# First norm of a two-block transformer kernel computed on token rows, with the raw tokens turned later

## The reference, cut to what matters

```python
def rmsnorm(x, g):
    xf = x.astype(jnp.float32)
    y = xf * lax.rsqrt(jnp.mean(xf * xf, axis=-1, keepdims=True) + EPS)
    return (y * g.astype(jnp.float32)).astype(x.dtype)
...
    h = jnp.concatenate([meta, x, zeros])        # 16 + 256 rows of 1024
    xn = rmsnorm(h, norm_mix_g[l])
    proj = xn @ w_in[l]                          # sb q,k,v and df q,k,v
    ...
    gates = sigmoid(xn @ w_gate[l] + b_gate[l])
    h = h + merged @ w_out[l]                    # needs the raw h again
```

## Time and profile before

| | us |
|---|---|
| median of 3 runs | 1934.32 (1933.79 to 1935.63) |
| profiled execution, its own time | 1935.6 |
| its span, first to last instruction | 1934.0 |
| TensorE busy | 1830.3 |
| VectorE busy | 799.9 |
| ScalarE busy | 595.1 |
| first matmul of unit 0 starts | 27.91 |

### The profile page before, as it was taken

How to read it: one execution, slowest core, us unless ns; L and a number is a source line. 1 busy time by engine, 2 the same in 40 slices (tenths; PEclk the granted TensorE clock), 3 DMA queues, 4 the chain that set the end, 5 groups by cost and what they waited for, 6 DMA issues and landing times.

```text
span 1934.0 us, 27605 instructions
## 1 busy us (share of the span) xinstructions
PE 1830.3 (95%) x11191; PEld 1225.8 (63%) x11192; DVE 799.9 (41%) x1359; ACT 595.1 (31%) x952; POOL 34.5 (2%) x61
## 2 busy tenths in 40 slices
PE   5999999989998999999999999999999999999996
PEld 5777878989998899899844344344344343343442
DVE  4344655868885554546422122122122122122222
ACT  4665777443434455565410000000000000000001
POOL 1000000000000000000000000000000000000000
PEclk8999999989998999999889999999999999999998
DMA  6323334768883744435849999999999999999994
GB/s 211 127 96 109 110 109 152 253 206 266 280 313 118 253 156 153 164 120 175 300 182 418 428 428 428 429 428 429 429 428 428 429 428 428 428 428 429 428 428 209
DMA packets 147813, 568.65 MB, mean 294 GB/s; under 512 B 6016, under 2 KB 102376, under 8 KB 123040
## 3 DMA queue, kind: packets, MB, share of 16 engines
q1 hardware_dynamic: 139616, 536.60, 70.5%
q0 software_dynamic: 8128, 31.07, 4.7%
HBM read 566.58 MB, written 3.43 MB: 295 GB/s over the span
## 4 chain that ended last, share of the span: by engine, by line
PE 58%; DMA 33%; ACT 4%; DVE 3%; issue 1%; SPq 0%; DVEq 0%
DMA s_ring<-in_w_mlp 33%; PE banks L2024 10%; PE banks L1644 9%; PE banks L1646 8%; PE banks L1645 8%; PE banks L1783 3%; PE banks L1784 3%; PE banks L1785 3%; PE banks L2061 3%; PE banks L2034 2%; PE banks L1611 1%; PE banks L2009 1%; ACT r_w2h L703 1%; DVE s_W L1066 1%; DVE r_w2l L1087 1%
## 5 line engine op out<-in xcount | busy, mean ns | idle before, releaser
L2024 PE MATMUL banks<-s_ring,s_W 128*64 128x512 f32 x2048 | 460.9, 598 | 29.8 <-DMA s_ring<-in_w_mlp 29.8
L2024 PEld LDWEIGHTS banks<-s_ring,s_W 128*64 128x64 f32 x2048 | 139.1, 137 | 332.3 <-issue 258.0
L1027 ACT ACTIVATE s_W<-s_W 128x512 f32<-128x512 f32 x32 | 20.2, 630 | 764.8 <-DVE s_W L1527 764.8
L2061 PE MATMUL banks<-s_ring,s_W 128*64 128x512 f32 x1024 | 227.4, 597 | 0.3 <-ACT s_W L1020 0.3
L1519 DVE TENSOR_TENSOR s_W<-banks,s_W 128x512 f32<-128x512 f32 x32 | 22.1, 691 | 462.5 <-PE banks L2061 462.5
L2061 PEld LDWEIGHTS banks<-s_ring,s_W 128*64 128x64 f32 x1024 | 73.6, 138 | 148.4 <-issue 133.9
L1087 DVE TENSOR_TENSOR r_w2l<-s_ring,r_w2h 128x1024 fp32r<-128x1024 f32 x88 | 107.5, 1224 | 106.9 <-ACT r_w2h L703 106.5
L1301 DVE TENSOR_TENSOR r_w2l<-s_ring,r_w2h 128x1024 fp32r<-128x1024 f32 x96 | 116.9, 1223 | 83.5 <-ACT r_w2h L875 83.3
L1506 DVE TENSOR_TENSOR s_W<-banks,s_W 128x512 f32<-128x512 f32 x128 | 82.1, 683 | 148.4 <-PE banks L2009 148.4
L1644 PE MATMUL banks<-r_x2h,r_w2h 128*128 128x256 f32 x448 | 130.8, 292 | 6.2 <-DVE r_x2l L1317 6.2
L2034 PEld LDWEIGHTS banks<-s_W 128*128 128x128 f32 x1024 | 120.0, 196 | 24.2 <-issue 24.2
(11 more groups left out here) (399 smaller groups left out, 3233.2 us busy)
## 6 DMA issues: line engine op xcount, KB each, us to landing
s_ring<-in_w_mlp SPq DMA_DIRECT2D x192, 2048.0 KB, 22.4
s_ring<-in_w_in SPq DMA_DIRECT2D x62, 1024.0 KB, 5.1
s_ring<-in_w_ada POOLq DMA_DIRECT2D x24, 1024.0 KB, 9.2
s_ring<-in_w_ffn_gate SPq DMA_DIRECT2D x11, 1024.0 KB, 5.5
s_ring<-in_w_ffn_up SPq DMA_DIRECT2D x11, 1024.0 KB, 10.6
s_ring<-in_w_ffn_down SPq DMA_DIRECT2D x5, 2048.0 KB, 9.9
s_ring<-in_w_gate SPq DMA_DIRECT2D x8, 1024.0 KB, 5.3
s_ring<-in_w_br_sb SPq DMA_DIRECT2D x4, 1024.0 KB, 4.9
```

The costliest lines, as they stand in the source:

```text
L2024: last = mm(pb[b][64 * h:64 * h + 64, :], XgT[:, 2 * c + k, :], slot(c, 2)[:, k, 1024 * h + 512 * b:1024 * h + 512 * b + 512], start=False ...
L2061: last = mm(pb[2][64 * h:64 * h + 64, :], aT[:, k, 64 * c:64 * c + 64], slot(4 + c, 4)[:, k, 512 * h:512 * h + 512], start=c == 0 and k == ...
```

## The change

The sums of squares are taken where the tokens lie as rows. ScalarE squares the first 128 rows with an accumulated sum, and the 16 meta rows; VectorE does the second 128 rows as a product and a reduction (`ssq`). ScalarE takes one Sqrt of the three columns, with the table loaded by a Sqrt of a constant at the start; VectorE takes the reciprocal (`rrow`). The rows are scaled as they lie: ScalarE group 0, VectorE group 1 (`xs`), GpSimd the meta rows (`xsm`). TensorE then turns the scaled rows, into banks 4, 6, 7 and 3 (tile t in half t // 4 of bank number t % 4 of that list). ScalarE rounds from PSUM with the gain as scale, VectorE forms the low part from PSUM in one instruction; meta goes by bank 5 and a small buffer `xnm`. The raw tokens, which the residual needs, are turned later, by `turn_raw(b)` ahead of units 1 to 4 on TensorE and `keep_raw(b)` on VectorE. The wait of `w_ada` is now for the last of these. The matmuls with ones are gone from the first norm, and counts of later waits shift by it.

```diff
@@ gpsimd
-        pool.wait_ge(S["gemm1"], 2)
+        pool.wait_ge(S["row_r"], 3)
+        nc.gpsimd.tensor_scalar(xsm, mtok, rrow[0:M, 2:3], None, ALU.mult).then_inc(S["x_meta"], 1)
+        pool.wait_ge(S["x_turned"], 10)
@@ scalar
-        for t in range(KT):
-            act.wait_ge(S["x_kept"], 1 + t // 2 + 1)
-            square(hT[:, :, :], sqa, TM, t)
-
-        act.wait_ge(S["x_turned"], 6)
+        act.wait_ge(S["filled"], 1)
+        act.activation(sml[:, 48:49], onec, ACT.Sqrt)
+        act.wait_ge(S["x_in"], 32)
+        act.activation(xs[:, 0, :], xtok[:, 0, :], ACT.Square, accum_out=ssq[:, 0:1]).then_inc(S["row_r"], 1)
+        act.wait_ge(S["norm_ms"], 1)
+        act.activation(xsm, mtok, ACT.Square, accum_out=ssq[0:M, 2:3]).then_inc(S["row_r"], 1)
+        act.wait_ge(S["row_r"], 2)
+        act.wait_ge(S["norm_ms"], 2)
+        act.activation(rrow, ssq, ACT.Sqrt, bias=epsc, scale=1.0 / D).then_inc(S["norm_r"], 1)
+        act.wait_ge(S["row_r"], 3)
+        act.activation(xs[:, 0, :], xtok[:, 0, :], ACT.Copy, scale=rrow[:, 0:1]).then_inc(S["row_r"], 1)
+        act.wait_ge(S["x_turned"], 1)
...
-        for n in range(2):
-            high1(n)
-        act.wait_ge(S["filled"], 1)
-        root(0, rms, TM)
+        high1(0)
+        act.wait_ge(S["vec_kept"], 1)
         for t in range(KT):
-            act.wait_ge(S["norm_x"], t + 1)
-            act.activation(xnh[:, t, :], xn[:, t, :], ACT.Copy).then_inc(S["xn_hi"], 1)
+            act.wait_ge(S["x_turned"], 2 + t % 4)
+            if t >= 4:
+                act.wait_ge(S["xn_lo"], t - 3)
+            if t == 4:
+                high1(1)
+            g = VROW["norm_mix_g"] + t
+            act.activation(xnh[:, t, M:TM], normed(t), ACT.Copy, scale=vec[:, g:g + 1]).then_inc(S["xn_hi"], 1)
+        act.wait_ge(S["norm_x"], 1)
+        act.activation(xnh[:, :, 0:M], xnm, ACT.Copy).then_inc(S["xn_hi"], 1)
         high1(2)
@@ vector
-        for b in range(5):
-            dve.wait_ge(S["x_turned"], b + 1)
-            if b == 0:
-                last = nc.vector.tensor_copy(hT[:, :, 0:M], pb[4][:, 0:P].rearrange("p (a n) -> p a n", a=KT))
-            else:
-                last = nc.vector.tensor_copy(hx[:, 2 * b - 2:2 * b, :], pb[b - 1].rearrange("p (a n) -> p a n", a=2))
-            last.then_inc(S["x_kept"], 1)
-        dve.wait_ge(S["x_kept"], 5)
+        st.do(nc.vector.memset(ssq[:, 2:3], 1.0))
+        st.wait()
+        dve.sem_inc(S["norm_ms"], 1)
+        dve.wait_ge(S["x_in"], 32)
+        st.do(tt(xsq, xtok[:, 1, :], xtok[:, 1, :], ALU.mult))
+        st.wait()
+        nc.vector.tensor_reduce(ssq[:, 1:2], xsq, AX.X, ALU.add).then_inc(S["norm_ms"], 1)
+        dve.wait_ge(S["cst_in"], 16)
+        dve.wait_ge(S["norm_r"], 1)
+        nc.vector.reciprocal(rrow, rrow).then_inc(S["row_r"], 1)
+        dve.wait_ge(S["row_r"], 3)
+        ts(xs[:, 1, :], xtok[:, 1, :], rrow[:, 1:2], None, ALU.mult).then_inc(S["row_r"], 1)
...
+        def keep_raw(b):
+
+            dve.wait_ge(S["x_turned"], 7 + b)
+            bank = pb[(4, 6, 7, 3)[b]].rearrange("p (a n) -> p a n", a=2)
+            nc.vector.tensor_copy(hx[:, 2 * b:2 * b + 2, :], bank).then_inc(S["x_kept"], 1)
@@ tensor
-        for d in range(KT):
-            last = nc.tensor.transpose(pb[4][:, M * d:M * d + M], mtok[:, P * d:P * d + P], ident[0:M, 0:M])
-        last.then_inc(S["x_turned"], 1)
-        for b in range(4):
+
+        def turn_raw(b):
+            pe.wait_ge(S["xn_lo"], b + 5)
             for j in range(4):
-                d, t = 2 * b + j // 2, j % 2
-                last = nc.tensor.transpose(pb[b][:, P * j:P * j + P], xtok[:, t, P * d:P * d + P], ident)
+                t = j % 2
+                last = nc.tensor.transpose(normed(b + j // 2 * 4)[:, P * t:P * t + P], xtok[:, t, P * (2 * b + j // 2):P * (2 * b + j // 2) + P], ident)
             last.then_inc(S["x_turned"], 1)
-        pe.wait_ge(S["filled"], 1)
-        pe.wait_ge(S["x_kept"], 5)
-        norm(0, sqa, TM)
+
         pe.wait_ge(S["vec_in"], 16 * len(VEC_ROWS))
         nc.tensor.transpose(pb[5][:, 0:NVEC], vrow, ident[0:NVEC, 0:NVEC]).then_inc(S["x_turned"], 1)
+        pe.wait_ge(S["row_r"], 5)
+        for b in range(4):
+            for d in (b, b + 4):
+                for t in range(2):
+                    last = nc.tensor.transpose(normed(d)[:, P * t:P * t + P], xs[:, t, P * d:P * d + P], ident)
+            last.then_inc(S["x_turned"], 1)
+        pe.wait_ge(S["vec_kept"], 1)
+        pe.wait_ge(S["x_meta"], 1)
+        for d in range(KT):
+            at = P + M * d
+            last = nc.tensor.transpose(pb[5][:, at:at + M], xsm[:, P * d:P * d + P], ident[0:M, 0:M])
+        last.then_inc(S["x_turned"], 1)
```

More of the change, by code:

```diff
@@ L293, in program @@
     rms = lent[:, 2176:2176 + TM]
-    xn = area(W, 16768, KT, TM)
+    xnm = area(W, 16768, KT, M)
+    ssq, rrow = sml[:, 56:59], sml[:, 60:63]
+    xs, xsm, xsq = area(lent, 0, 2, D), lent[0:M, 2048:2048 + D], lent[:, 3072:3072 + D]
     xnh, xnl = rounded("xnh", False, 0, KT, TM), rounded("xnl", True, 5632, KT, TM)
@@ L396, in program @@
         "x_turned", "x_kept", "vec_kept", "filled", "lam_sum", "lam_exp", "csil",
-        "norm_sq", "norm_ms", "norm_r", "norm_x", "norm_s",
+        "row_r", "x_meta", "norm_sq", "norm_ms", "norm_r", "norm_x", "norm_s",
         "gemm1", "act_evac1", "dve_evac1", "gate_done", "gemm2", "act_evac2", "dve_evac2", "gab_done", "rg_exp",
@@ L496, in down_group, with normed @@
         return slot(4 + (kk // 4 + 1) % 2, 4)[:, kk % 4:kk % 4 + 1, :]
+    def normed(t):
+        return pb[(4, 6, 7, 3)[t % 4]][:, T * (t // 4):T * (t // 4) + T]
     def since(eng, name, n):
@@ L646, in _ @@
         pool.wait_ge(S["up_step"], 3 * FT)
-        pool.wait_ge(S["norm_x"], 16)
+        pool.wait_ge(S["norm_x"], KT + 1)
         pool.wait_ge(S["ada_sum"], KT * ADAS)
@@ L682, in root @@
         def root(k, r, n):
-            act.wait_ge(S["norm_ms"], k + 1)
+            act.wait_ge(S["norm_ms"], k + 2)
             st.do(act.activation(r[:, 0:n], pb[3][:, 0:n], ACT.Ln, bias=epsc, scale=1.0 / D))
@@ L834, in _ @@
         for t in range(KT):
-            act.wait_ge(S["norm_x"], 2 * KT - KT + t + 1)
+            act.wait_ge(S["norm_x"], t + 2)
             act.activation(xfh[:, t, :], xf[:, t, :], ACT.Copy).then_inc(S["x_hi"], 1)
@@ L883, in _ @@
         for t in range(KT):
-            act.wait_ge(S["norm_x"], 2 * KT + t + 1)
+            act.wait_ge(S["norm_x"], KT + t + 2)
             square(hx, sqa, T, t)
@@ L887, in _ @@
         for t in range(KT):
-            act.wait_ge(S["norm_x"], 3 * KT + t + 1)
+            act.wait_ge(S["norm_x"], 2 * KT + t + 2)
             act.activation(x2h[:, t, :], xn2[:, t, :], ACT.Identity, bias=modT[:, t:t + 1]).then_inc(S["x_hi"], 1)
@@ L985, in _ @@
         for t in range(KT):
-            act.wait_ge(S["norm_x"], 4 * KT + t + 1)
+            act.wait_ge(S["norm_x"], 3 * KT + t + 2)
             act.activation(hn[:, t, :], hn[:, t, :], ACT.Identity, bias=modT[:, 24 + t:25 + t]).then_inc(S["norm_s"], 1)
@@ L1088, in low1 @@
                    ALU.subtract).then_inc(S["w1_lo"], 1)
-        for n in range(2):
-            low1(n)
-        norm(0, xn, hT, rms[:, 0:TM], vrows("norm_mix_g"))
+        low1(0)
         for t in range(KT):
             dve.wait_ge(S["xn_hi"], t + 1)
-            tt(xnl[:, t, :], xn[:, t, :], xnh[:, t, :].bitcast(F32), ALU.subtract).then_inc(S["xn_lo"], 1)
+            g = VROW["norm_mix_g"] + t
+            stt(xnl[:, t, M:TM], normed(t), vec[:, g:g + 1], xnh[:, t, M:TM].bitcast(F32), ALU.mult, ALU.subtract).then_inc(S["xn_lo"], 1)
+            if t == 4:
+                low1(1)
+        dve.wait_ge(S["x_turned"], 6)
+        tt(xnm, pb[5][:, P:2 * P].rearrange("p (a n) -> p a n", a=KT), vrows("norm_mix_g").unsqueeze(2).broadcast_to([P, KT, M]), ALU.mult)\
+            .then_inc(S["norm_x"], 1)
+        dve.wait_ge(S["xn_hi"], KT + 1)
+        tt(xnl[:, :, 0:M], xnm, xnh[:, :, 0:M].bitcast(F32), ALU.subtract).then_inc(S["xn_lo"], 1)
         low1(2)
+        def keep_raw(b):
+            dve.wait_ge(S["x_turned"], 7 + b)
+            bank = pb[(4, 6, 7, 3)[b]].rearrange("p (a n) -> p a n", a=2)
+            nc.vector.tensor_copy(hx[:, 2 * b:2 * b + 2, :], bank).then_inc(S["x_kept"], 1)
         dve.wait_ge(S["lam_in"], 64)
@@ L1232, in _ @@
                 low1(h + 3)
+                if 1 <= h <= 4:
+                    keep_raw(h - 1)
                 for g in UNITS1[h]:
@@ L1606, in _ @@
         mm = nc.tensor.matmul
+        pe.wait_ge(S["filled"], 1)
         def add_square(k, buf, n, t):
-            pe.wait_ge(S["norm_sq"], KT * k + t + 1)
+            pe.wait_ge(S["norm_sq"], KT * (k - 1) + t + 1)
             last = mm(pb[3][:, 0:n], ones[:, :], buf[:, t, 0:n], start=t == 0, stop=t == KT - 1)
@@ L1695, in sb_step @@
                     pe.wait_ge(S["sb_zs"], h)
+                else:
+                    pe.wait_ge(S["x_kept"], 4)
                 q = sqT[:, h, :]
```

(6 more changed lines are left out.)

1 line of the change is left out of this document (removed).

## The result

The changed kernel takes 1924.83 us (median of 5 runs, 1924.68 to 1928.2) against 1934.32 (median of 5, 1932.47 to 1936.96): ratio 0.9949, with a 95% interval from 0.9937 to 0.9961. It is faster by 9.5 us. Forecast were 1925.0 and 9.3. The profiled execution took 1924.68 us, with a span of 1923.0.

The account below looks back on a forecast made before the run. TensorE was taken to set the pace of the dense stages, expert weights that of the last half. Unit 4's result 9.9 us earlier, less 0.6 for handoffs, gave 9.3: 1934.3 - 9.3 = 1925.0 us, own range 1924.0 to 1926.4, wider range 1923.0 to 1929.5.

Parts of the forecast that it names:

- last low token tile: VectorE's last low part of the normed tokens, which unit 0 on TensorE needs, ready at 21.4 us.
- turns of raw tokens: Four raw turns on TensorE between units 1 to 4, 16 transposes of 0.11: 1.8 us at full clock, 3.5 at low.
- U4: Start of ScalarE's taking of unit 4's result: forecast 35.2 us against 45.15, 9.9 us earlier before 0.6 was taken off.
- the deduction for handoffs: 0.6 us taken off the 9.9 us gain for some ten handoffs not counted, leaving 9.3.
- the full level from about 18.5: TensorE works from 13.0 us with no gap over 1.5, so full clock from about 18.5 and no loss behind it.
- the slow pace of the transposes: TensorE's 16 scaled-token transposes taken at 0.22 us each, the lower clock level; at full clock 1.8 us earlier.
- The rival in which transposes don't raise the clock: Turning leaves TensorE's clock low, so units 0 and 1 lose 1.5 to 3 us: 1926.5 to 1928; chance 0.10.
- The meta hold: GpSimd's scaled meta rows reach TensorE late, at 19.5 to 22, costing 1.5 to 4 us: 1926.5 to 1929.5; chance 0.28.
- my bounds: GpSimd's scaling of the meta rows ends between 13.5 and 14.8 us, leaving 2 us before TensorE wants them.
- My price for a late row: Meta rows late for TensorE cost nothing up to 18 us, from there one for one.
- Given back: The start gains but a later stage, late unit splits or expert weights, loses it: 1933 to 1934.5; chance 0.05.
- One for one: What the start gains reaches the end in full, since SyncE issues expert weights as TensorE's steps release the ring.

Follow-up runs that it names:

- the second trace: Repeat of an unchanged kernel: the changed kernel, 1925.26 us, ratio 0.9948; where the kernel before is meant, 1935.59 us in one run.

## Why the prediction was right

*The sum, step by step.* Squares done 11.35, measured 11.25; root done 11.9, measured 11.9; turning from 13.0, measured 13.16; meta transposes at 16.7, measured 16.77; unit 0 from 17.7, measured 17.73; last low token tile 21.4, measured 21.48. The turns of raw tokens are smaller than I took them, 0.45 each: from unit 2's result to unit 4's it is 6.71 us (28.91 to 35.62) in place of 5.87 (39.28 to 45.15), so 0.42 each. In all U4 at 35.62 against 35.2 before the deduction for handoffs, and 35.8 with it. What took the 0.4 was not handoffs but the clock, at the end of unit 0: the last low tile is there at 21.48 and TensorE, still behind from the low level, takes it at 21.86; with the clock up early, in the second trace, it is there at 21.28 and taken at 21.40. Unit 0's last matmul ends at 22.37, where I had 21.8. No run puts back the sums of squares by themselves, so the share of each part of the change is shown only for the root, the roundings, the raw turns and GpSimd.

*What failed is the clock.* I wrote "I expect the full level from about 18.5 and no loss behind it". The first half does not hold: 21.1 in one trace, about 16 in the other. The second does but for the 0.4 us just named. The run with idle multiplications prices all low pace at the start at 1.7 us, which I had in the sum as the slow pace of the transposes. The rival in which transposes don't raise the clock falls: in the run with raw tokens turned early there is nothing else on TensorE, and the second batch is at full pace. That speaks against the rule of the Trainium skill that I had weighed ("TensorE: Matmul & The Clock Gate", Part 4: PE-mode transpose).

*The meta hold* did not occur: rows ready at 15.43, wanted at 16.77. GpSimd's 3.40 us lay outside my bounds all the same (13.5 to 14.8 for the end), and the slack was 1.3 us and not 2. My price for a late row was too low: rows at 21.12 cost 4.4 us, where I had let them cost nothing up to 18 and one for one from there, so 3.1.

*Given back* does exist, by a way that I had not seen: the stretch after 520 us, 4 us long or short by the clock. Both first traces had the short case, so it cancelled there. "One for one" is thus not what a single pair of traces shows: in the first pair 9.5 us at U4 are 11.0 at the end, in the second 12.1 are 7.0.

*Some luck.* The trace of before that I worked from had its sums of squares at the full level. From the second trace the same sum would have given a gain of 47.36 - 35.8 = 11.6 us. The two traces of before and the two of after are 9.5 to 12.1 apart at U4, and 8.3 to 9.0 (each kernel's first with first, second with second) at 630 us. The medians say 9.5 and 10.2. So the mechanism is settled and its size to some 2 us; the agreement within 0.2 us is not a measure of how well such a sum can be made; about 2 us is.

## What to carry to other kernels

A norm at the start of a program is a chain of handoffs during which the big engine stands idle: sum the squares in the layout in which the data lie, choose root functions that need no table load between the sums and the scaling (here 3 to 4 us), and move everything that the first matmul does not need behind it, or better into the idle time ahead of it. Before reading a time off one trace, look at whether the clock was at the same level there in a second execution. A gain of 3 us at the start can be lost 500 us later without any wait changing, so give the landmark and the total, both.

## What the runs showed of the hardware

- The time at which the clock rises at the start differs by some 5 us between executions of the same code, though TensorE's work begins at the same moment (13.16 and 13.26 us: rise at 21.1 and about 16).
- At the start the granted clock's column reads 1.00 while the spacing is that of the low level (15 matmuls of 256 columns in 3 us). Later the column and the spacing agree: 0.50 and 0.21 us in unit 0 of the kernel before.
- Transposes alone brought the full level: with 12 from 8.69 and one at 12.16, those from 12.98 ran at it.
- Two stretches of this program take one of two lengths in different executions of the same code: the one behind the 352 matmuls (some 103 or 107 us) and the last 32 matmuls of 512 columns (7.9 to 8.7 or 9.2 to 9.4 us).
- GpSimd scales 16 x 1024 elements in 2.83 us, 3.40 the first time; VectorE does it in 0.73.
- ScalarE needs 0.48 us for 128 x 256 from PSUM with a scale per partition, and VectorE 0.48 for scaling and subtraction in one; from SBUF ScalarE's rounding takes 0.42.
- Square, Ln and Exp in a row took three table loads of 1.28 us, one each.
